# Two attentions of a three-block network: order of TensorE's steps, division on GpSimd, sink as a key column

## The chip, the cores and the metric

One Trainium2 chip, one of its cores. The metric is the device time of the one launch in microseconds; lower is better. The kernel is written in a low-level language: for each engine (TensorE, VectorE, ScalarE, GpSimd, SyncE) its own program, held together by counting semaphores.

## The reference, cut to what matters

Three blocks in a row. The first convolves, the second holds a windowed attention over 512 tokens and 256 context tokens, the third a sliding-window attention (6 heads), an attention over 256 memory tokens (4 heads) and a recurrent mixer; each is followed by a convolving feed-forward part. What the change touches, for one head of 64 (q, k, v), with a sink s:

```python
logits = q @ k.T * 64 ** -0.5              # + mask or bias, -inf outside the window
m = max(max(logits), s)
e = exp(logits - m)
p = e / (sum(e) + exp(s - m))              # the memory heads have no sink
out = p @ v
```

## The kernel before, in words

Weights stream in pieces from memory through SyncE's queue, are split into a high and a low part (ScalarE, GpSimd) and multiplied in three products each. Between these streams stand the two attentions: the first (ATT1) after the stream `qkv` and ahead of `wo`, the second (ATT2) after `w_in`, followed by the mixer's preparation (`rw_pre`).

An attention is a list of **units**: one block of 128 queries of one head. ATT1 has 64 units in 16 groups of 4 (`groups1`, L2250): for each of 4 key heads 4 blocks of queries, each with 4 query heads. A unit of the first and last block has 512 keys (256 of the window and 256 of the context), one of the middle blocks 640. So 512, 640, 640, 512 follow each other, four units each. ATT2 has 24 units in 4 groups of 6 (128 keys in the first group, then 256) and 16 units of the memory heads in 4 groups of 4, with 256 keys (`groups2`, L2670). The 128 columns more or less are those of the band.

What each engine does for a unit u:
- TensorE, `att_pe` (L1976): `scores` (L1979), in the fast 32-bit form, with the high and low part of the keys, the masks or the bias, into one of two pairs of PSUM banks. It waits until the exponential of u-2 is done (`att_p`). `turn` (L1987) transposes the probabilities in squares of 128 into one of three banks, a piece at a time. `values` (L2003) multiplies a whole group's transposed probabilities with the values, in full 32-bit form, with outputs of 64 rows in either half of the array; it is cut into four quarters, each in a step of its own.
- VectorE, `att_dve` (L2043): `negated` takes the maximum and multiplies it by -1/8 (in ATT1 with the sink as the other bound); `inverse` adds the sink's exponential in ATT1, takes the reciprocal and divides the row of probabilities; copies of transposed pieces marked "D"; `low`, the low part of a group's result.
- ScalarE, `att_act` (L2083): `exps`, in ATT1 the sink's exponential first, then that of the row, with its sum; copies of the pieces marked "A" (all in ATT1, every second unit in ATT2); `high_part` of a group's result.
- GpSimd has no part in it. Ahead of ATT2's stretch it has six operations of `rw_pre_pool` (L2940).

The order is written out by hand: each engine runs a loop over steps u, and the constants of L1943 say by how many steps a part lags behind the scores. TensorE's step u is: scores of u+2, `turn` of u-1, then a quarter of the values of a group whose last unit is u-2 to u-5. Each engine works through its queue in order.

ATT2's band units already carry the sink as two extra columns of the scores (`sk2`, L2562), of which one is used. In ATT1 the sink is a column of its own (`sinks`, `nsk`).

Of the kernel before, what the change touches and what calls it, by code (L numbers as in the profile page):

```python
# [6 lines left out]
P = 128  # L7
D = 1024
KD = D // P
SEQ = 512  # L10
# [5 lines left out]
HD = 64  # L16
TAPS = 31
# [77 lines left out]
def constants():  # L95
# [19 lines left out]

    sin = sin * np.repeat(np.array([-1, 1, 1, -1], np.float32), HD // 2)[:, None]
    q, k = np.arange(P)[:, None], np.arange(P)[None]
# [33 lines left out]
class Program:  # L151


    def __init__(self, nc, ctx, A):
# [42 lines left out]
        self.sm_max = at("sm_max", region(64), [4])  # L197
        self.sm_neg = at("sm_neg", region(64), [4])
        self.sm_sum = at("sm_sum", region(64), [4])
        self.sm_rd = at("sm_rd", region(64), [4])  # L200
        self.sm_e = at("sm_e", region(64), [4])
# [65 lines left out]
        self.nsk = nxt("nsk", [16])  # L267
# [5 lines left out]
        self.p1 = nxt("p1", [3, 648])  # L273
# [3 lines left out]
        self.p2 = nxt("p2", [3, 264])  # L277
# [100 lines left out]
def build_in(nc, ctx, A, out, stop):  # L378
# [77 lines left out]
    att_p = sem("att_p")  # L456
    att_n = sem("att_n")
# [1079 lines left out]
    zero_col = M.one[:, 2:3]  # L1537

# [386 lines left out]
    class Unit:  # L1925
# [5 lines left out]
        def __init__(self, scores, nk, parts, place, at=0, sink=None):  # L1931
            self.scores, self.nk, self.at, self.sink = scores, nk, at, sink
            self.parts, self.place = parts, place

# [6 lines left out]
    SCALE = HD ** -0.5  # L1941
    TURN_BANK, OUT_BANK = 4, 7
    TURN, VALUES, OUT_A, OUT_D, HIGH, LOW = 1, 2, 2, 3, 6, 7  # L1943

    class Attention:
# [26 lines left out]

        def turn_ps(self, j):
            return (TURN_BANK + j % 3) * 512

    def att_pe(pe, X, first=None):  # L1976
# [10 lines left out]
        def turn(u):  # L1987
            x = X.units[u]
            pe.wait_ge(att_n, done(X.u0 + u + 1))
            for m, (k0, nk, _) in enumerate(x.parts):  # L1990
# [7 lines left out]
                for k in range(0, nk, P):  # L1998
                    mm = pe.transpose(M.ps[:, X.turn_ps(j) + k:X.turn_ps(j) + k + P],
                                      X.p[:, u % 3, k0 + k:k0 + k + P], ident)  # L2000
                mm.then_inc(att_t, 1)

        def values(g, quarter):  # L2003
            grp, e = X.groups[g], X.last[g]
            if quarter == 0:
# [5 lines left out]
            for o, v, rhs, first, last in todo[quarter * len(todo) // 4:(quarter + 1) * len(todo) // 4]:  # L2011
                mm = pe.matmul(o, v, rhs, start=first, stop=last, skip_group_check=True)  # L2012
            if quarter == 3:
                mm.then_inc(att_o, 1)
# [1529 lines left out]
```

## Time and profile before

| what | value |
|---|---|
| median of three runs | 2412.74 us (2409.75 to 2416.72) |
| the profiled execution, its own time | 2414.43 us |
| its span | 2412.6 us |
| TensorE busy | 2258.1 us (94%) |
| VectorE, ScalarE, GpSimd busy | 1170.6, 994.5, 859.1 us |
| mean granted TensorE clock | 0.963 |

How to read it: busy times are of instructions, and TensorE's matmuls overlap, so its share is no measure of its speed. The loads of weights (PEld) give a better beat: one belongs to each matmul. A granted clock of 1.00 is 2.4 GHz, 0.50 is 1.2 GHz. `ps` is PSUM, `p` a row of probabilities, `pt` the transposed ones, `sm_...` the small columns of a row's maximum, sum and reciprocal.

### The profile page before, as it was taken

The numbers are of one execution on the slowest core, as the hardware profiler recorded it, in microseconds if no ns is written. First come the engines' busy times: TensorE is split into PE (matmuls) and PEld (weight loads), VectorE is DVE, ScalarE is ACT, GpSimd is POOL, SyncE is SP. The second block draws the span as 40 slices with busy tenths as digits, with TensorE's granted clock in tenths as the row PEclk, the third lists the DMA queues.
The fourth block names the chain that finished last, engine by engine and source line by source line (L and its number), as shares of the span: only waits on it lengthen the run. The fifth ranks groups of instructions, "written<-read, shape, count | busy, mean of one in ns | idle before, by whom it ended". The sixth has DMA issues, their size and how long they took to land.

```text
span 2412.6 us, 37223 instructions
## 1 busy us (share of the span) xinstructions
PE 2258.1 (94%) x14399; PEld 1868.9 (77%) x14399; DVE 1170.6 (49%) x2044; ACT 994.5 (41%) x1685; POOL 859.1 (36%) x449
## 2 busy tenths in 40 slices
PE   4999598999999998999989999989988889999998
PEld 3888487888888887877778888877746777878877
DVE  3699824332033325678433223458465436540541
ACT  5666544332133314588444324444353213441441
POOL 1699324223223324400244444433301113444443
PEclk8999898999999998999989999999888989999999
DMA  8778011222122221300123333332200002332332
GB/s 274 254 255 274 25 53 53 61 62 74 57 61 61 71 70 55 96 19 1 45 88 96 102 90 96 102 105 79 83 1 1 2 2 70 102 103 84 97 106 83
DMA packets 337730, 205.96 MB, mean 85 GB/s; under 512 B 5997, under 2 KB 335287, under 8 KB 337591
## 3 DMA queue, kind: packets, MB, share of 16 engines
q1 hardware_dynamic: 331915, 193.83, 26.9%
q10 hardware_dynamic: 5676, 10.24, 1.4%
q8 instruction: 93, 1.52, 0.3%
q14 instruction: 46, 0.38, 0.1%
HBM read 200.28 MB, written 2.19 MB: 84 GB/s over the span
## 4 chain that ended last, share of the span: by engine, by line
PE 72%; issue 11%; POOL 5%; DVE 5%; ACT 3%; DVEq 1%; SPq 1%; DMA 1%; ACTq 1%; POOLq 0%
PE ps L621 21%; PE ps L622 21%; PE ps L623 21%; POOL w_lo L548 2%; POOL pc L1608 2%; DVE ps L1576 1%; PE ps L894 1%; PE ps L1984 1%; PE ps L2012 1%; ACT w_hi L591 1%; DVE m L3214 1%; PE ps L3013 1%; DMA ada_x<-in_ada_w 1%; PE ps L1668 0%; SPq L772 0%
## 5 line engine op out<-in xcount | busy, mean ns | idle before, releaser
L548 POOL TENSOR_TENSOR w_lo<-raw,w_hi 128x1024 fp32r<-128x1024 f32 (+1 forms) x203 | 526.2, 2593 | 1073.4 <-ACT w_hi L591 1056.8
L621 PE MATMUL ps<-x_hi,w_hi 128*128 128x512 f32 (+1 forms) x1896 | 686.5, 362 | 35.1 <-DVE x_lo L1479 14.0
L622 PE MATMUL ps<-x_lo,w_hi 128*128 128x512 f32 (+1 forms) x1896 | 676.2, 357 | 0.0
L623 PE MATMUL ps<-x_hi,w_lo 128*128 128x512 f32 (+1 forms) x1896 | 674.9, 356 | 0.0
L591 ACT ACTIVATE w_hi<-raw 128x1024 fp32r<-128x1024 f32 (+1 forms) x251 | 280.6, 1118 | 615.8 <-PE ps L623 610.5
L621 PEld LDWEIGHTS ps<-x_hi,w_hi 128*128 128x128 f32 x1896 | 365.1, 193 | 100.0 <-issue 22.8
L622 PEld LDWEIGHTS ps<-x_lo,w_hi 128*128 128x128 f32 x1896 | 365.5, 193 | 50.0 <-issue 1.7
L623 PEld LDWEIGHTS ps<-x_hi,w_lo 128*128 128x128 f32 x1896 | 364.7, 192 | 50.5
L1858 DVE SCALAR_TENSOR_TENSOR f_a<-ps,prm,f_a 128x511 f32<-128x511 f32 (+2 forms) x176 | 116.2, 681 | 378.5 <-ACT f_b L1820 367.6
L621 PE MATMUL ps<-g_hi,w_hi 128*128 128x512 f32 (+1 forms) x704 | 256.8, 365 | 3.9 <-DVE g_lo L1867 1.7
L622 PE MATMUL ps<-g_lo,w_hi 128*128 128x512 f32 (+1 forms) x704 | 255.7, 363 | 0.0
L623 PE MATMUL ps<-g_hi,w_lo 128*128 128x512 f32 (+1 forms) x704 | 255.3, 363 | 0.0
L574 POOL TENSOR_TENSOR w_lo<-raw,w_hi 128x1024 fp32r<-128x1024 f32 x50 | 119.6, 2394 | 209.8 <-ACT w_hi L591 209.8
L1576 DVE SCALAR_TENSOR_TENSOR ps<-vp,prm,ps 128x512 f32<-128x512 f32 x320 | 169.4, 617 | 3.5 <-PE ps L956 3.5
L621 PEld LDWEIGHTS ps<-g_hi,w_hi 128*128 128x128 f32 x704 | 132.8, 189 | 26.7 <-DVE g_lo L1867 4.6
L623 PEld LDWEIGHTS ps<-g_hi,w_lo 128*128 128x128 f32 x704 | 132.7, 188 | 21.0
L622 PEld LDWEIGHTS ps<-g_lo,w_hi 128*128 128x128 f32 x704 | 132.8, 189 | 20.2
L1820 ACT ACTIVATE f_a<-ps,prm 128x512 f32<-128x512 f32 (+1 forms) x66 | 55.8, 845 | 211.0 <-PE ps L623 209.0
L621 PE MATMUL ps<-xg_hi,w_hi 128*128 128x512 f32 x352 | 137.7, 391 | 2.4 <-POOL w_lo L548 2.4
L1608 POOL TENSOR_TENSOR pc<-pc,pt 128x768 f32<-128x768 f32 x72 | 132.5, 1840 | 17.5 <-ACT pt L1597 10.6
L622 PE MATMUL ps<-xg_lo,w_hi 128*128 128x512 f32 x352 | 137.0, 389 | 0.0
L623 PE MATMUL ps<-xg_hi,w_lo 128*128 128x512 f32 x352 | 137.0, 389 | 0.0
(384 smaller groups left out, 2969.3 us busy)
## 6 DMA issues: line engine op xcount, KB each, us to landing
raw<-in_ffn_w_up SPq DMA_DIRECT2D x88, 512.0 KB, 3.8
ada_tail<-in_ada_w SPq DMA_DIRECT2D x22, 1024.0 KB, 7.4
raw<-in_ffn_w_down SPq DMA_DIRECT2D x32, 704.0 KB, 4.6
raw<-in_w_up SPq DMA_DIRECT2D x44, 512.0 KB, 3.8
ada_s<-in_ada_w SPq DMA_DIRECT2D x20, 1024.0 KB, 7.9
raw<-in_conv_w_pw SPq DMA_DIRECT2D x24, 512.0 KB, 6.3
raw<-in_w_down SPq DMA_DIRECT2D x16, 704.0 KB, 4.6
raw<-in_w_in SPq DMA_DIRECT2D x17, 512.0 KB, 3.9
```

The costliest lines, as they stand in the source:

```text
L548: pool.tensor_tensor(M.w_lo[:, slot, 0:K * P], M.raw[:, slot, 0:K * P], M.w_hi[:, slot, 0:K * P].bitcast(F32), ALU.subtract).then_inc(lo_r ...
L574: pool.tensor_tensor(M.w_lo[:, slot, 0:K * P], M.raw[:, slot, 0:K * P], M.w_hi[:, slot, 0:K * P].bitcast(F32), ALU.subtract).then_inc(lo_r ...
L591: act.activation(M.w_hi[:, slot, 0:K * P], M.raw[:, slot, 0:K * P], ACT.Copy).then_inc(hi_ready, 1)
L621: pe.matmul(o, wh, hi[:, k, t0:t0 + tn], start=first, stop=False)
L622: pe.matmul(o, wh, lo[:, k, t0:t0 + tn], start=False, stop=False)
L623: return pe.matmul(o, wl, hi[:, k, t0:t0 + tn], start=False, stop=last)
L894: mm = pe.matmul(M.ps[32 * q:32 * q + 32, at:at + P], M.sc32[:, k, :], weights[q // 2][:, k, q % 2 * P:(q % 2 + 1) * P], start=(k == 0), s ...
L1576: dve.scalar_tensor_tensor(out=o, in0=src, scalar=w, in1=o, op0=ALU.mult, op1=ALU.add)\
L1608: pool.tensor_tensor(acc, acc, M.pt[:, m % PT_RING, :], ALU.add).then_inc(pool_tap, 1)
L1820: ins = act.activation(dst[:, slot, 0:w], M.pair(pr, 0, w), ACT.Identity, scale=ffn_cols(b, zero_tap, t, hf, j), bias=ffn_cols(b, None, t, ...
L1858: ins = dve.scalar_tensor_tensor(out=dst[:, slot, o0:o1], in0=M.pair(pr, o0 + sh, o1 + sh), scalar=ffn_cols(b, tap, t, hf, j), in1=dst[:, ...
L1984: mm = pe.matmul(M.pair(u % 2, off, off + n), lhs, rhs, start=first, stop=True, skip_group_check=True)
```

## The change

- TensorE's step is now: a piece of values, `turn` of u-3, scores of u+2. The values of a group come in two pieces, in steps L+5 and L+6 for the group's last unit L.
- Lags: TURN 3 (1), OUT_A 3 (2), OUT_D 4 (3), VALUES 5 (2); HIGH 6 and LOW 7 stay. There are five rows of probabilities (3) and eight small columns (4).
- The factor 1/8 is put into the tables and scales of the queries, so that the exponential has a scale of 1 and the maximum is negated by the reduction itself.
- ATT1's sink becomes a column of the scores (one more matmul with two columns), as in ATT2; its exponential and the sum drop out.
- The reciprocals are taken for two units at once, every second step, and GpSimd divides (`att_pool`).
- In ATT1 the piece of the 256 context keys is copied by VectorE, that of the band by ScalarE.

```diff
-    TURN, VALUES, OUT_A, OUT_D, HIGH, LOW = 1, 2, 2, 3, 6, 7
+    TURN, OUT_A, OUT_D, VALUES, PIECES_V, HIGH, LOW = 3, 3, 4, 5, 2, 6, 7
...
-        for u in range(n_u + VALUES + 3):
+        for u in range(n_u + VALUES + PIECES_V):
+            for piece in range(PIECES_V):
+                for g in X.groups_at(u, VALUES + piece):
+                    values(g, piece)
+            if 0 <= u - TURN < n_u:
+                turn(u - TURN)
             if u + 2 < n_u:
                 scores(u + 2)
-            if 0 <= u - TURN < n_u:
-                turn(u - TURN)
-            for quarter in range(4):
-                for g in X.groups_at(u, VALUES + quarter):
-                    values(g, quarter)
...
         def negated(u):
-            x, b = X.units[u], u % 4
+            x, b = X.units[u], u % 8
             dve.wait_ge(att_s, done(X.u0 + u + 1))
-            dve.tensor_reduce(M.sm_max[:, b:b + 1], M.pair(u % 2, x.at, x.at + x.nk), AX.X, ALU.max)
-            dve.drain()
-            if x.sink:
-                dve.tensor_scalar(M.sm_neg[:, b:b + 1], M.sm_max[:, b:b + 1], -SCALE, x.sink[1], ALU.mult, ALU.min)\
-                    .then_inc(att_m, 1)
-            else:
-                dve.tensor_scalar(M.sm_neg[:, b:b + 1], M.sm_max[:, b:b + 1], -SCALE, None, ALU.mult).then_inc(att_m, 1)
+            dve.tensor_reduce(M.sm_neg[:, b:b + 1], M.pair(u % 2, x.at, x.at + x.nk), AX.X, ALU.max, negate=True)\
+                .then_inc(att_m, 1)
         def inverse(u):
-            x, b = X.units[u], u % 4
-            dve.wait_ge(att_p, done(X.u0 + u + 1))
-            if x.sink:
-                dve.tensor_tensor(M.sm_sum[:, b:b + 1], M.sm_sum[:, b:b + 1], M.sm_e[:, b:b + 1], ALU.add)
-                dve.drain()
-            dve.reciprocal(M.sm_rd[:, b:b + 1], M.sm_sum[:, b:b + 1])
-            dve.drain()
-            p = X.p[:, u % 3, 0:x.nk]
-            dve.tensor_scalar(p, p, M.sm_rd[:, b:b + 1], None, ALU.mult).then_inc(att_n, 1)
+            b = u % 8
+            dve.wait_ge(att_p, done(X.u0 + u + 2))
+            dve.reciprocal(M.sm_rd[:, b:b + 2], M.sm_sum[:, b:b + 2]).then_inc(att_r, 1)
...
             if u < n_u:
                 negated(u)
-            if 0 <= u - 1 < n_u:
-                inverse(u - 1)
             if 0 <= u - OUT_D < n_u:
                 bring_out(dve, dve.tensor_copy, X, u - OUT_D, "D", att_t, att_ed)
+            if u % 2 == 0 and 0 <= u - 2 < n_u:
+                inverse(u - 2)
...
-            if x.sink:
-                act.activation(M.sm_e[:, b:b + 1], M.sm_neg[:, b:b + 1], ACT.Exp, scale=1.0, bias=x.sink[0])
-            act.activation(X.p[:, u % 3, 0:x.nk], M.pair(u % 2, x.at, x.at + x.nk), ACT.Exp, scale=SCALE,
+            act.activation(X.slot(u)[:, 0:x.nk], M.pair(u % 2, x.at, x.at + x.nk), ACT.Exp, scale=1.0,
...
+    def att_pool(pool, X):
+        for u, x in enumerate(X.units):
+            pool.wait_ge(att_r, done((X.u0 + u) // 2 + 1))
+            p = X.slot(u)[:, 0:x.n_keys]
+            pool.tensor_scalar(p, p, M.sm_rd[:, u % 8:u % 8 + 1], zero_col, ALU.mult, ALU.add).then_inc(att_n, 1)
...
-                    scores += [(SEQ, CTX, q, M.k_hi[:, g, SEQ:TOK], True), (SEQ, CTX, q, M.k_lo[:, g, SEQ:TOK], False)]
+                    scores += [(SEQ, CTX, q, M.k_hi[:, g, SEQ:TOK], True), (SEQ, CTX, q, M.k_lo[:, g, SEQ:TOK], False),
+                               (TOK, 2, M.fr[:, P:2 * P], M.sk1[:, h, :], True)]
...
-                    heads.append(Unit(scores, nk, [(0, nb, "A"), (nb, CTX, "A")], place, at,
-                                      (M.sinks[:, h:h + 1], M.nsk[:, h:h + 1])))
+                    heads.append(Unit(scores, nk, [(0, nb, "A"), (nb, CTX, "D")], place, at))
...
             if name == "w_out":
                 low_stream(pool, name, 0, 2)
                 rw_pre_pool(pool)
+                att_pool(pool, ATT2)
...
+            if name == "wo":
+                low_stream(pool, name, 0, 2)
+                att_pool(pool, ATT1)
                 low_stream(pool, name, 2, 8)
```

Outside the attentions: the two last of the ten rotated tiles of `qkv` (the keys) take the factor back with scalar_tensor_tensor in place of tensor_tensor, the sinks of ATT1 are split once into a high and a low part (`sk1`, two small operations), the queries of ATT2 get their factor through the scale and bias of a square root, and the bias table is copied without a factor.

## Rows read from the trace of the kernel before

**Rows 1.** Busy time per engine and granted clock (PEclk) in four stretches.
```profile
1025.48:1169.22 143.74, 137.15 (x940) 99.42 (x940) 113.68 (x336) 116.79 (x339) 2.38 (x1) 0.98 0.03 9
1733.06:1797.16 64.10, 56.10 (x299) 36.74 (x300) 48.12 (x187) 32.39 (x108) 5.39 (x6) 0.88 0.03 9
1772.00:1775.00 3.00, 3.00 (x12) 1.34 (x12) 1.90 (x9) 1.32 (x5) 0.00 (x0) 0.52 0.02 5
1777.00:1788.00 11.00, 9.10 (x46) 4.79 (x45) 9.70 (x38) 6.72 (x22) 0.00 (x0) 1.00 0.00 1
```

**Rows 2.** Waits from 1040 to 1150: total, times, longest in us.
```profile
PEld ps L1984 <- issue: 16.5, 43, 0.4
```

**Rows 3.** TensorE's weight loads, first attention: start, us, count; scores L1984, transposes L1999, values L2012.
```profile
1041.68 0.19 PEld L1984 LDWEIGHTS ps<-k_hi,q 128*128 128x128 f32 x1 [0.62 <-ACTq L2095]
...
1042.50 0.57 PEld L1999 LDWEIGHTS ps<-kb,p 128*128 128x128 f32 x5
...
1093.48 0.20 PEld L2012 LDWEIGHTS ps<-pt,vt 128*64 128x64 f32 x4 [0.17 <-issue]
1094.06 0.19 PEld L1984 LDWEIGHTS ps<-k_hi,q 128*128 128x128 f32 x1 [0.39 <-ACTq L2095]
...
1095.29 0.62 PEld L2012 LDWEIGHTS ps<-pt,vt 128*64 128x64 f32 x6 [0.17 <-issue]
1096.29 0.19 PEld L1984 LDWEIGHTS ps<-k_hi,q 128*128 128x128 f32 x1 [0.38 <-issue]
...
1096.89 0.47 PEld L1999 LDWEIGHTS ps<-kb,p 128*128 128x128 f32 x4
```

**Rows 4.** The same: scores of unit 13, scores of unit 61, first product of wo.
```profile
1054.72 0.19 PEld L1984 LDWEIGHTS ps<-k_hi,q 128*128 128x128 f32 x1 [0.39 <-issue]
...
1154.58 0.19 PEld L1984 LDWEIGHTS ps<-k_hi,q 128*128 128x128 f32 x1 [0.39 <-issue]
...
1169.22 0.19 PEld L621 LDWEIGHTS ps<-x_hi,w_hi 128*128 128x128 f32 x1 [1.39 <-DVE x_lo L2071]
```

**Rows 5.** Second attention: a sink's matmul and what follows; units 16, 22, 39.
```profile
1750.92 0.19 PEld L1984 LDWEIGHTS ps<-sk,fr 128*128 128x128 f32 x1
1751.06 0.20 PEld L1999 LDWEIGHTS ps<-kb,p 128*128 128x128 f32 x2
...
1754.77 0.19 PEld L1984 LDWEIGHTS ps<-k_hi,pj_r 128*128 128x128 f32 x1 [0.35 <-issue]
...
1763.70 0.19 PEld L1984 LDWEIGHTS ps<-k_hi,pj_r 128*128 128x128 f32 x1 [0.35 <-issue]
...
1788.58 0.19 PEld L1984 LDWEIGHTS ps<-x_hi 128*128 128x128 f32 x1 [0.81 <-ACTq L2095]
```

**Rows 6.** Groups by form in both attentions: count | busy us, mean ns | idle before.
```profile
L2093 ACT ACTIVATE p<-ps,sm_neg 128x640 f32<-128x640 f32 x32 | 24.9, 779 | 0.0
L2049 DVE TENSOR_REDUCE sm_max<-ps 128x1 f32<-128x512 f32 x32 | 22.1, 689 | 12.7 <-PE ps L1984 12.4
L2093 ACT ACTIVATE p<-ps,sm_neg 128x512 f32<-128x512 f32 x32 | 21.7, 679 | 0.0
L2103 ACT ACTIVATE x_hi<-ps 128x256 fp32r<-128x256 f32 x16 | 6.2, 385 | 6.5 <-PE ps L2012 6.3
...
L2943 POOL TENSOR_SCALAR behind<-pj,prm,one 128x512 f32<-128x512 f32 x3 | 2.3, 766 | 0.4 <-DVE pj L2623 0.4
L2103 ACT ACTIVATE x_hi<-ps 128x384 fp32r<-128x384 f32 x4 | 2.0, 492 | 3.6 <-PE ps L2012 3.6
```

**Rows 7.** Timeline at the start of the second attention: rw_pre on GpSimd, a reduction.
```profile
1733.96 1.04 POOL L2945 TENSOR_TENSOR behind<-behind 128x512 f32<-128x512 f32 x1
...
1734.33 0.29 DVE L2049 TENSOR_REDUCE sm_max<-ps 128x1 f32<-128x129 f32 x1 [1.32 <-PE ps L1984]
...
1737.72 1.04 POOL L2945 TENSOR_TENSOR behind<-behind 128x512 f32<-128x512 f32 x1
```

**Rows 8.** Timeline: the copy behind the transposes of 1096.89.
```profile
1097.42 0.38 ACT L2098 ACTIVATE pt<-ps 128x256 f32<-128x256 f32 x1 [0.27 <-PE ps L1999]
```

More of the change, by code:

```diff
@@ L16 @@
 HD = 64
+SCALE = HD ** -0.5
 TAPS = 31
@@ L272, in __init__ @@
         o = self.mod_rows_at
-        self.p1 = nxt("p1", [3, 648])
+        p1 = nxt("p1", [3, 648])
+        self.p1 = [p1[:, i, :] for i in range(3)] + [t[:, :] for t in p1_more]
         self.pt1 = nxt("pt1", [2, 5 * 4 * P])
@@ L276, in __init__ @@
         o = r_s
-        self.p2 = nxt("p2", [3, 264])
+        p2 = nxt("p2", [3, 264])
+        self.p2 = [p2[:, i, :] for i in range(3)] + [at(f"p2_{3 + i}", r_raw + i * w + behind_8, [264])[:, :] for i in (0, 1)]
         self.pt2 = nxt("pt2", [2, 2 * 6 * P])
@@ L456, in build_in @@
     att_p = sem("att_p")
+    att_r = sem("att_r")
     att_n = sem("att_n")
@@ L1537, in build_in @@
     zero_col = M.one[:, 2:3]
+    eps_q_col = M.one[:, 4:5]
     VLAT, VCTX = PAD, SEQ + 3 * PAD
@@ L1925, in build_in, with __init__ @@
     class Unit:
-        def __init__(self, scores, nk, parts, place, at=0, sink=None):
-            self.scores, self.nk, self.at, self.sink = scores, nk, at, sink
+        def __init__(self, scores, nk, parts, place, at=0):
+            self.scores, self.nk, self.at = scores, nk, at
             self.parts, self.place = parts, place
+            self.n_keys = sum(n for _, n, _ in parts)
     class Group:
@@ L1971, in groups_at, with slot @@
             return [g for g, e in enumerate(self.last) if e + lag == u]
+        def slot(self, u):
+            return self.p[u % len(self.p)]
         def turn_ps(self, j):
@@ L1999, in turn, with values @@
                     mm = pe.transpose(M.ps[:, X.turn_ps(j) + k:X.turn_ps(j) + k + P],
-                                      X.p[:, u % 3, k0 + k:k0 + k + P], ident)
+                                      X.slot(u)[:, k0 + k:k0 + k + P], ident)
                 mm.then_inc(att_t, 1)
-        def values(g, quarter):
+        def values(g, piece):
             grp, e = X.groups[g], X.last[g]
-            if quarter == 0:
+            if piece == 0:
                 pe.wait_ge(att_ea, done(X.ea0 + X.brought_a[e]))
@@ L2010, in values @@
             todo = list(grp.products(X.pt[:, g % 2, :]))
-            for o, v, rhs, first, last in todo[quarter * len(todo) // 4:(quarter + 1) * len(todo) // 4]:
+            for o, v, rhs, first, last in todo[piece * len(todo) // PIECES_V:(piece + 1) * len(todo) // PIECES_V]:
                 mm = pe.matmul(o, v, rhs, start=first, stop=last, skip_group_check=True)
-            if quarter == 3:
+            if piece == PIECES_V - 1:
                 mm.then_inc(att_o, 1)
@@ L2214, in qkv_dve @@
             dve.wait_ge(rope_r, done(n + 1))
-            dve.tensor_tensor(M.gate[:, n % 2, 0:SEQ], ps, kf_cos, ALU.mult)
+            if n < 8:
+                dve.tensor_tensor(M.gate[:, n % 2, 0:SEQ], ps, kf_cos, ALU.mult)
+            else:
+                dve.scalar_tensor_tensor(out=M.gate[:, n % 2, 0:SEQ], in0=ps, scalar=1.0 / SCALE, in1=kf_cos,
+                                         op0=ALU.mult, op1=ALU.mult)
             dve.tensor_tensor(rope_ps(n)[a, :], ps[b, :], kf_sin[b, :], ALU.mult)
@@ L2222, in qkv_dve @@
             else:
-                dve.tensor_tensor(M.k_[:, n - 8, 0:SEQ], rope_ps(n), M.gate[:, n % 2, 0:SEQ], ALU.add).then_inc(rope_c, 1)
+                dve.scalar_tensor_tensor(out=M.k_[:, n - 8, 0:SEQ], in0=rope_ps(n), scalar=1.0 / SCALE,
+                                         in1=M.gate[:, n % 2, 0:SEQ], op0=ALU.mult, op1=ALU.add).then_inc(rope_c, 1)
             if n == 5:
-                dve.tensor_scalar(M.nsk[:, :], M.sinks[:, 0:16], -1.0, None, ALU.mult).then_inc(fr_ready, 1)
+                dve.wait_ge(fr_ready, done(1))
+                dve.scalar_tensor_tensor(out=M.sk1[HD:P, :, :], in0=M.sinks[HD:P, 0:16].unsqueeze(2)
+                                         .to_broadcast([HD, 16, 2]), scalar=1.0 / HD,
+                                         in1=M.sk1[HD:P, :, :].bitcast(F32), op0=ALU.mult, op1=ALU.subtract)\
+                    .then_inc(fr_ready, 1)
             if 1 <= n <= 8:
@@ L2663, in w_in_dve @@
                 for n in range(3):
-                    ins = dve.scalar_tensor_tensor(out=M.bias_lo[:, 2 * n:2 * n + 2, :], in0=halves(odd(BIAS_BANK[n])),
-                                                   scalar=1.0 / SCALE, in1=M.bias[:, 2 * n:2 * n + 2, :].bitcast(F32),
-                                                   op0=ALU.mult, op1=ALU.subtract)
+                    ins = dve.tensor_tensor(M.bias_lo[:, 2 * n:2 * n + 2, :], halves(odd(BIAS_BANK[n])),
+                                            M.bias[:, 2 * n:2 * n + 2, :].bitcast(F32), ALU.subtract)
                 V_S.mark(ins, "blo")
```

46 lines of the change are left out of this document (27 added, 19 removed).

## The prediction

> **What bounds the kernel now.** I read the stretches first, then the waits, the timeline of TensorE and the durations by form. The two attentions last 143.7 and 64.1 us of the span of 2412.6 [rows 1]. Outside them the change touches only a few small operations, so the answer lies in these 208 us. In the first one TensorE shows busy for 137 us, ScalarE for 117, VectorE for 114. In its middle 110 us TensorE's score loads pause for 16.5 us with nothing to wait for ("issue") [rows 2]: TensorE bounds it, with pauses of its own.
>
> The pauses have a pattern. A unit with 512 keys (A) takes 0.60 us of scores and 0.46 of transposes, then 0.17 of pause and a piece of value products; one with 640 (B) takes 0.82 and 0.57 [rows 3]. A piece of 4 instructions lasts 0.58 to the next load, one of 6 lasts 1.00: 0.42 per slot (the two column halves run beside each other) and 0.16 fixed. So a piece costs 0.33 us besides its products, where the tile shape goes to 128*64 and back. Sixteen units (8 A, 8 B, in 4 groups) come to 8 x 1.42 (scores) + 8 x 1.03 (transposes) + 16 x 0.33 + 20 slots x 0.42 = 33.3 us. Units 13 to 61 are three such periods: 99.86 us, 33.3 each [rows 4]. The sum holds.
>
> **The change on TensorE.** Two pieces per group in place of four save 8 x 0.33 = 2.6 us a period. The sink's column costs one more matmul per unit, 0.14 us from its load to the next in the second attention, which has it already [rows 5]: 2.2 us. A period is then 32.9: only 0.4 less.
>
> **The other engines.** VectorE loses the product with -1/8, the addition of the sink's exponential, half the reciprocals and the division; it gains the copy of the 256 context keys. ScalarE loses the sink's exponential and that copy. None of it is time where TensorE bounds. The division goes to GpSimd, idle here: 0.77 us for 512 elements in the same form [rows 6]. For 640 it is at least that and at most 0.96, in proportion. Against 1.8 us and more per unit it is covered and I take it at zero: the transposes wait two steps longer than before. Without cover it would show first in step L+8 (L the last unit of a group), where the pair's reciprocals stand some 1.5 us ahead of its first transposes; one division of 0.96 fits. VectorE is not slowed by it: its reduction of 129 elements at 1734.33 takes 0.29 while GpSimd works from 1733.96 on [rows 7].
>
> **The new wait.** With TURN and OUT_A at 3, ScalarE's step u is: exponential of u, copy of unit u-3. That copy needs the transposes which TensorE makes in its own step u, behind a value piece. The next exponential is queued behind the copy, and scores u+3 wait for that exponential. It decides in step L+6, where ScalarE also makes the high part. From the end of the transposes: 0.07 to the copy (transposes 1096.89 plus 0.46, copy 1097.42), copy 0.33 (0.43 for 384), high part 0.39, exponential with its accumulator 0.77 or 0.87, and 0.08 to TensorE [rows 6, 8]: 1.64 (A) or 1.84 (B). TensorE meanwhile has one unit's scores and transposes, 0.74 + 0.46 = 1.20 or 0.96 + 0.57 = 1.53. It stalls for 0.44 or 0.31 us, 0.38 a group, 1.5 a period. Bounds: zero, if ScalarE turns out to have more room; 0.9 a group, if each of the five links comes 0.1 later. In steps without values the loop of scores, reduction (0.69) and exponential needs 1.25 us a unit (A), which TensorE needs too: no more stall.
>
> **First attention.** Per period -0.4 + 1.5 = +1.1, three times: +3.3. Start: values begin in step 8, not 5, and the chain to the exponential lacks two small instructions; followed with these durations, unit 13 comes 2.4 us earlier. End: what was put off has to be done. Unit 61 to the first product of wo lasts 14.6 us before [rows 4]. After, three units' scores, five units' transposes, the last pieces of groups 13, 14 and 15, one stall, and the last high and low part make 16: +1.4. Sum +2.3.
>
> **Second attention.** Six operations of rw_pre stand on GpSimd ahead of the first division and end at 1738.76 [rows 7]: unit 6 comes 0.5 us later; then the later start of the values gives back, and unit 16 comes 1.8 us earlier in all. Six band units take 8.93 us (units 16 to 22) [rows 5]. After: on TensorE 6 x 0.79 + 2 x 1.17 = 7.1; the wait above costs 1.0 (one unit is only 0.79 of work, against 0.07 + 0.33 + 0.49 for the high part of 384 [rows 6] + 0.64 + 0.25 until the other engines are in step); smaller waits for copies and reductions 0.6: 8.7, so -0.2. The four units of a memory head are only 4.2 us of TensorE, but ScalarE's chain of copy, high part, exponential, copy, exponential makes 6.3. Units 22 to 39 come to 25.1 us against 24.9 [rows 5], which hold a stretch at half clock (0.52) [rows 1] that I take as gone. Sum -1.8 - 0.2 + 0.2 and an unchanged end, rounded: -1.6, as followed.
>
> The scales folded into tables, the keys' sums as scalar_tensor_tensor and the copy of the sinks lie beside the weight products of qkv and w_in: zero, at most 0.5 us without that cover.
>
> **Sum.** 2.3 - 1.6 = +0.7 us. The profiled execution took 2414.4 us (span 2412.6 and 1.8 around it), 1.7 above the median of three runs, 2412.74. From the median: **2413.4 us**. A measurement can tell about 0.3%, 7.2 us, from no change, so this is no change. Its own range is 2407 to 2420: with the bounds of the stalls, 14 groups x -0.38 or +0.5.
>
> **Rivals.** *TensorE alone* (faster): ScalarE is never late. Then the stalls go: 14 x 0.38 = 5.3 in the first attention, 3 x 1.6 and 3 x 2.1 in the second, 16.4 in all: 2397. For it: ScalarE has 27 us free in the first [rows 1]. Against: its order, not its load, holds it. It decides once half of this is won, below 2405. Chance 0.26.
>
> *Half clock in the memory groups* (slower): TensorE there would pause for 2 us in 6.3. The trace shows that it comes in this very place: from 1772 to 1775 the grant is 0.52, the lower of the two levels [rows 1]. At it two pieces of 1.17 last 2.0 and the other 1.8 us up to twice as long: +3.5 a group, 2424 with three groups. It decides from two groups on. Against: from 1777 to 1788 memory groups ran at the full clock, with weight loads busy for only 4.8 of 11 us [rows 1]. Chance 0.16. The Trainium skill (TensorE: Matmul & The Clock Gate, A second HAM failure mode: psum-queue depth-cycling) says that TensorE, when it pauses shortly and often between groups of matmuls, swings between its two clocks; by that rule this would be the likelier rival.
>
> **Numbers.** Forecast 0.58, rivals 0.26 and 0.16. Of the forecast little passes 0.3% on either side. Faster 0.27, same 0.56, slower 0.17. The range of 2402 to 2422 leaves out the farther half of both rivals.
>
> **What would show it.** Right: a period of 16 units near 34.4 us; pieces of 1.00 and 1.43 with the same pauses; once a group, in step L+6, scores that wait 0.3 to 0.5 us for ScalarE; GpSimd at some 0.8 us a unit with nobody waiting for it; unit 13 two us earlier, wo two us later; a memory group of 6.3 us. Wrong: a period below 33, transposes that wait for GpSimd, or a longer stretch at half clock in the second attention than before.

## The result and the profile after

The changed kernel took 2418.01 us (median of 20 runs, 2408.91 to 2420.88), the kernel before beside it 2411.57. The ratio is 1.0017 with a 95% interval of 1.0009 to 1.0025, or about +4 us (the two medians alone lie 6.4 us apart, because the changed kernel's times fall into two clusters, 5 below 2412 and 15 above 2416): within the 0.3% that the prediction calls no change, and inside its range of 2402 to 2422. The profiled execution took 2419.05 us (span 2417.2).

So the number was right. The parts were not: the first attention became shorter, not longer, and what the change lost it lost where the prediction had put nothing. From the first instruction of each stage on TensorE to the next, in the profiled executions:

| stage | before | after | forecast | found |
|---|---|---|---|---|
| up to the first attention | 1025.48 | 1026.94 | 0 | +1.5 |
| first attention | 143.74 | 141.62 | +2.3 | -2.1 |
| wo and feed-forward to w_in | 430.64 | 431.37 | 0 | +0.7 |
| w_in | 133.20 | 136.51 | 0 | +3.3 |
| second attention | 63.99 | 64.69 | -1.6 | +0.7 |
| the rest | 615.55 | 616.07 | 0 | +0.5 |
| span | 2412.6 | 2417.2 | +0.7 | +4.6 |

The two attentions of the changed kernel, stretches as in [rows 1] (us, then busy time of PE, PEld, DVE, ACT, POOL, the granted clock, the DMA's share and GB/s):

```profile
1026.94:1168.56 141.62, 134.71 (x1004) 108.82 (x1004) 80.53 (x176) 83.08 (x211) 54.17 (x65) 0.96 0.03 8
1736.44:1801.13 64.69, 54.88 (x298) 38.05 (x298) 28.14 (x87) 30.64 (x107) 26.69 (x46) 0.85 0.03 9
```

VectorE and ScalarE lost 33 and 34 us in the first one, and the attention became 2 shorter: neither bounded it by its load. Its waits from 1040 to 1150, as [rows 2] (waiter, releaser, total, times, longest):

```profile
PEld ps L2008 <- issue: 6.9, 18, 0.4
PEld ps L1993 <- ACTq L2092: 5.2, 19, 0.4
PEld ps L2008 <- POOL p L2114: 3.1, 8, 0.4
```

Before, the pauses had no releaser, 16.5 us of them ahead of the scores alone; in the same stretch 10.0 are left (first and third row), and the scores (L1993) wait for ScalarE's exponential (L2092) instead. The wait on GpSimd (L2114) is in the place of the pause behind a value piece and of its length, so it costs nothing.

Weight loads of the changed kernel, as [rows 3] and [rows 4]: the second step with values (piece, transposes, scores), the two steps behind it, then scores of units 13 and 61 and the first product of wo.

```profile
1054.84 0.19 PEld L1993 LDWEIGHTS ps<-k_hi,q 128*128 128x128 f32 x1 [0.43 <-ACTq L2092]
...
1090.80 1.05 PEld L2021 LDWEIGHTS ps<-pt,vt 128*64 128x64 f32 x10
1092.24 0.53 PEld L2008 LDWEIGHTS ps<-kb,p 128*128 128x128 f32 x5 [0.38 <-issue]
1092.74 0.19 PEld L1993 LDWEIGHTS ps<-k_hi,q 128*128 128x128 f32 x1
...
1093.45 0.53 PEld L2008 LDWEIGHTS ps<-kb,p 128*128 128x128 f32 x5
1094.34 0.19 PEld L1993 LDWEIGHTS ps<-k_hi,q 128*128 128x128 f32 x1 [0.35 <-ACTq L2092]
...
1095.65 0.19 PEld L1993 LDWEIGHTS ps<-k_hi,q 128*128 128x128 f32 x1 [0.19 <-ACTq L2092]
...
1152.15 0.19 PEld L1993 LDWEIGHTS ps<-k_hi,q 128*128 128x128 f32 x1 [0.19 <-ACTq L2092]
...
1168.56 0.19 PEld L626 LDWEIGHTS ps<-x_hi,w_hi 128*128 128x128 f32 x1 [1.39 <-DVE x_lo L2070]
```

Units 13 to 61 take 97.31 us, 32.4 a period (forecast 34.4; before 33.3). Read the distances. A piece of ten loads to the transposes takes 1.44 (forecast 1.43). Five transposes to the next scores take 0.50 at 1092.24, but 0.89 at 1093.45: a stall of 0.39, where the forecast had 0.44 in this very place, the step behind ScalarE's step L+6. Over a period this first stall is 0.39 twice, where the scores are those of 512 keys, and 0.27 twice, where they are those of 640. What holds it is ScalarE's queue:

```profile
1092.83 0.49 ACT L2095 ACTIVATE pt<-ps 128x384 f32<-128x384 f32 x1 [1.57 <-PE ps L2008]
1093.22 0.38 ACT L2100 ACTIVATE x_hi<-ps 128x256 fp32r<-128x256 f32 x1
1093.48 0.70 ACT L2090 ACTIVATE p<-ps,sm_neg 128x513 f32<-128x513 f32 x1
1094.05 0.21 ACT L2090 ACTIVATION_READ_ACCUMULATOR p<-ps,sm_neg 128x1 f32 x1
```

ScalarE waits 1.57 us for the transposes, then copies, makes the high part, and only then comes the exponential that the scores of 1094.34 need: the five links of the prediction. The next step adds 0.22 that it did not have (0.61 for 0.39), in two of a period's four groups; in the other two it adds nothing.

GpSimd by forms in the first attention, for the forecast of 0.77 and at most 0.96:

```profile
L2114 POOL TENSOR_SCALAR p<-p,sm_rd,one 128x640 f32<-128x640 f32 x32 | 27.8, 880 | 35.0 <-DVE sm_rd L2065 35.0
L2114 POOL TENSOR_SCALAR p<-p,sm_rd,one 128x512 f32<-128x512 f32 x32 | 24.4, 773 | 46.4 <-DVE sm_rd L2065 46.4
```

### The profile page after: what moved, and what is told of

Its sections match the earlier page's. It is cut to its first block, busy times and chain, and to the rows that moved or that the text cites. A ratio compares the mean times of both kernels' runs of the same rounds, so it can differ in the third digit from the quotient of the medians.

```text
span 2417.2 us, 36779 instructions
## 1 busy us (share of the span) xinstructions
PE 2260.5 (94%) x14463; PEld 1884.5 (78%) x14463; DVE 1117.2 (46%) x1784; ACT 960.1 (40%) x1558; POOL 933.6 (39%) x554
## 4 chain that ended last, share of the span: by engine, by line
PE 79%; POOL 5%; DVE 5%; issue 4%; ACT 3%; ACTq 1%; DVEq 1%; DMA 1%; SPq 1%; POOLq 0%
PE ps L626 22%; PE ps L627 21%; PE ps L628 21%; PE ps L1993 3%; PE ps L2021 2%; POOL pc L1614 2%; PE ps L2008 2%; POOL w_lo L553 2%; DVE ps L1582 1%; PE ps L899 1%; ACTq L2092 1%; ACT w_hi L596 1%; DVE m L3230 1%; PE ps L3029 1%; DMA ada_x<-in_ada_w 1%
## 5 line engine op out<-in xcount | busy, mean ns | idle before, releaser
L1614 POOL TENSOR_TENSOR pc<-pc,pt 128x768 f32<-128x768 f32 x72 | 132.7, 1844 | 17.4 <-ACT pt L1603 10.5
```

The source lines that it names most:

```text
L1614: pool.tensor_tensor(acc, acc, M.pt[:, m % PT_RING, :], ALU.add).then_inc(pool_tap, 1)
```

## The experiments

My theory after the profile, before the runs: TensorE's own beat of a period is 30.6 us, and 1.8 of stalls stand on it, by ScalarE's order; outside the attentions nothing changed but the stretches at half clock. (The trace's record of the clock gives their lengths; a window's PEclk shows them as a share.) The rivals: the stalls come from the shortness of the steps without values; and the edits outside the attentions cost the missing time. All kernels were timed in five rounds beside the kernel before, 5 to 12 runs each: e1 to e4, e5 to e8 and e9 to e12 beside 34, 23 and 28 runs of it, with medians of 2411.76, 2412.74 and 2411.27, so medians of different groups compare by their ratios. "Period" is a third of the time from unit 13 to unit 61 in the kernel's own profile; the attentions run from first to first instruction as above.

| kernel | median us | ratio to before, 95% interval | period | first | second |
|---|---|---|---|---|---|
| changed, again (e3) | 2418.58 | 1.0022 (1.0013 to 1.0031) | 32.4 | 141.56 | 62.89 |
| before, again (e12) | 2411.69 | 1.0001 (0.9990 to 1.0011) | 33.3 | 143.78 | 63.46 |
| e1 high part first | 2406.82 | 0.9973 (0.9962 to 0.9983) | 31.7 | 138.65 | 57.31 |
| e4 VectorE divides | 2422.78 | 1.0038 (1.0027 to 1.0050) | 35.6 | 153.10 | 64.83 |
| e5 no sink in the first | 2412.06 | 0.9989 (0.9979 to 1.0000) | 32.2 | 139.54 | 63.16 |
| e6 transposes, values | 2411.67 | 0.9986 (0.9975 to 0.9996) | 32.5 | 142.06 | 59.21 |
| e7 four pieces | 2434.22 | 1.0081 (1.0065 to 1.0097) | 36.3 | 155.30 | 70.76 |
| e8 high first, one piece | 2397.95 | 0.9929 (0.9914 to 0.9945) | 30.3 | 133.43 | 56.12 |
| e9 high first, pair cut | 2403.25 | 0.9961 (0.9948 to 0.9974) | 30.9 | 135.48 | 57.64 |
| e2 outside edits alone | 2415.47 | 1.0011 (1.0000 to 1.0023) | 33.3 | 143.82 | 64.52 |
| e10 the first's share | 2415.61 | 1.0018 (1.0009 to 1.0028) | | 143.78 | 64.08 |
| e11 the second's share | 2412.43 | 1.0004 (0.9994 to 1.0014) | | 143.30 | 62.55 |

### e1: is it the order in ScalarE's queue?

```diff
+            for g in X.groups_at(u, HIGH):
+                high_part(g)
             if 0 <= u - OUT_A < n_u:
                 bring_out(act, copy, X, u - OUT_A, "A", att_t, att_ea)
-            for g in X.groups_at(u, HIGH):
-                high_part(g)
```

> The changed kernel with one edit: in ScalarE's step the high part of a group stands ahead of the copy, not behind it. In the changed kernel's profile ScalarE is late for the scores by 0.2 to 0.4 us in the two steps behind a group's pieces, 1.8 us in a period of 16 units (32.4 us). Theory A (the late exponential is the copy plus the high part queued ahead of it, as the prediction had it): the high part then runs while TensorE still transposes, the chain is shorter by 0.39, the stall of step L+6 goes and that of L+7 shrinks, a period takes 30.9 to 31.3 us and the first attention is 4 to 6 us shorter; with the clock's stretches as they are, median near 2413. Rival B (the stall is the short work of the two steps without values, whatever ScalarE's order): the period stays at 32.2 to 32.5 and the median at 2418.

The same step in its timeline of ScalarE:

```profile
1087.80 0.38 ACT L2100 ACTIVATE x_hi<-ps 128x256 fp32r<-128x256 f32 x1 [1.09 <-PE ps L2021]
1088.27 0.49 ACT L2095 ACTIVATE pt<-ps 128x384 f32<-128x384 f32 x1
1088.66 0.68 ACT L2090 ACTIVATE p<-ps,sm_neg 128x513 f32<-128x513 f32 x1
```

The high part now runs beside the transposes. The transposes that took 0.89 to the next scores take 0.61, and the period falls by 0.74 to 31.7: less than the 1.1 to 1.5 expected, since 0.1 to 0.3 of stall stays in six of the eight steps without values, 1.0 in all. The first attention becomes 3.0 us shorter, the second 5.6 to 7.4 (two profiles of the changed kernel, with one and two stretches at half clock there that e1's lacks, some 1.5 us each). Theory A holds, with a smaller size in the first attention; the second, where the chain is long against TensorE's work, gains most even without these stretches. That gain the expectation had not counted: its median was 2413, measured 2406.82. Against the kernel before, this order is 0.27% faster.

### e4: was GpSimd's division worth anything?

```diff
-            dve.reciprocal(M.sm_rd[:, b:b + 2], M.sm_sum[:, b:b + 2]).then_inc(att_r, 1)
+            dve.reciprocal(M.sm_rd[:, b:b + 2], M.sm_sum[:, b:b + 2])
+            dve.drain()
+            for v in (u, u + 1):
+                p = X.slot(v)[:, 0:X.units[v].n_keys]
+                dve.tensor_scalar(p, p, M.sm_rd[:, v % 8:v % 8 + 1], None, ALU.mult).then_inc(att_n, 1)
```

> The changed kernel with the division back on VectorE: behind the two reciprocals, every second step, it divides both rows itself (0.49 and 0.55 us each in the kernel before); GpSimd has no part in the attentions. VectorE's work a unit rises from about 1.3 to 1.8 us against 2.0 us of the beat. Theory A (GpSimd's part is needed, since the next reduction is queued behind two divisions and the scores' exponential behind it): the period in the first attention rises from 32.4 to 33.5 to 36 us, the median by 4 to 14 us. Rival B (VectorE has room enough, the division's place doesn't matter): the period stays within 0.3 us of 32.4 and the median at 2418.

VectorE in one group:

```profile
1092.54 0.15 DVE L2065 RECIPROCAL sm_rd<-sm_sum 128x2 f32<-128x2 f32 x1
1092.77 1.02 DVE L2069 TENSOR_SCALAR p<-p,sm_rd 128x640 f32<-128x640 f32 x2
1093.69 0.69 DVE L2058 TENSOR_REDUCE sm_neg<-ps 128x1 f32<-128x513 f32 x1
```

The reduction stands behind two divisions of 1.02 us, the exponential behind the reduction, and scores wait up to 1.0 us once a group. The period rises by 3.2 us to 35.6, the first attention by 11.5. The median rises by only 4.2 over e3, since these runs were granted more clock (0.960 to 0.967, e3's 0.958 to 0.961); how far that moves a time is measured under e12, and at equal clock the rise is about 11. So the cover that the prediction counted at zero is not free by itself: with these lags the division is free on GpSimd only.

### e5: what does the sink's column cost?

```diff
-                nk = CTX + nb + 1
+                nk = CTX + nb
...
-                scores += [..., (SEQ, CTX, q, M.k_lo[:, g, SEQ:TOK], False),
-                               (TOK, 2, M.fr[:, P:2 * P], M.sk1[:, h, :], True)]
+                scores += [..., (SEQ, CTX, q, M.k_lo[:, g, SEQ:TOK], False)]
```

> The changed kernel without the sink of the first attention: its column of the scores (one matmul of two columns a unit) and the 513th or 641st key are left out, so the outputs lack the sink there. From the changed kernel's profile a unit's scores take 0.71 (A) and 0.94 us (B) to the next load against 0.59 and 0.82 before: 0.12 a unit. Theory A (TensorE's beat counts in the eight steps with values, ScalarE's chain in the others): 8 x 0.12 = 1.0 us comes off the 32.4 of a period, the other eight give nearly nothing since the stall grows by what the scores lose; 31.3 to 31.6 a period, the first attention 3.5 to 5 us shorter. Rival B (TensorE's beat counts everywhere): 1.9 us off the period, 30.5, and 8 us off the attention.

e5 computes another result: its outputs lack the sink. Both theories miss: the period falls by only 0.2 us. Another 1.4 us come at the start, but there its profile has 6.8 us at half clock and both of the changed kernel have 10.2, so they are not the sink's alone. Its weight loads, a step without values and one with them:

```profile
1091.87 0.19 PEld L1993 LDWEIGHTS ps<-k_hi,q 128*128 128x128 f32 x1 [0.42 <-ACTq L2092]
...
1092.46 0.47 PEld L2008 LDWEIGHTS ps<-kb,p 128*128 128x128 f32 x4
1093.19 0.19 PEld L1993 LDWEIGHTS ps<-k_hi,q 128*128 128x128 f32 x1 [0.26 <-ACTq L2092]
...
1093.97 1.05 PEld L2021 LDWEIGHTS ps<-pt,vt 128*64 128x64 f32 x10
```

Scores take 0.78 to a value piece, with the sink 0.79: the same. To transposes they take 0.59 without and 0.71 with it. So in the steps with values the small matmul fits into a pause that is there without it (0.19), and in the others its 0.12 is taken back by the wait for ScalarE. The 2.2 us that the prediction charged a period are 1.0 on TensorE without its waits and 0.2 in the balance. The rows also price a piece behind scores where no sink fills the pause: 0.19 ahead of it (0.78 for 0.59) and 0.16 inside, 0.35.

### e6: what does the place of the piece cost?

```diff
+            if 0 <= u - TURN < n_u:
+                turn(u - TURN)
             for piece in range(PIECES_V):
                 for g in X.groups_at(u, VALUES + piece):
                     values(g, piece)
-            if 0 <= u - TURN < n_u:
-                turn(u - TURN)
```

> The changed kernel with the transposes of u-3 ahead of the piece of values, not behind it. In the kernel before transposes followed by a piece took 0.63 and 0.74 us, in the changed kernel transposes followed by scores 0.38 and 0.50, and scores followed by a piece 0.08 more than scores followed by transposes: so a piece behind transposes costs 0.17 more than one behind scores. Theory A: on TensorE a period gains 8 x 0.17 = 1.3 us; but ScalarE copies while the piece runs, so that the stall of step L+6 shrinks from 0.3 to at most 0.1 and that behind it too: 1.2 us less. The period stays at 32.0 to 32.8. Rival B (the place of the piece is free, only the number of pieces counts): TensorE gains nothing, the stall goes all the same, 30.9 to 31.3.

```profile
1091.34 0.53 PEld L2008 LDWEIGHTS ps<-kb,p 128*128 128x128 f32 x5
1092.03 1.05 PEld L2021 LDWEIGHTS ps<-pt,vt 128*64 128x64 f32 x10 [0.17 <-issue]
1093.47 0.19 PEld L1993 LDWEIGHTS ps<-k_hi,q 128*128 128x128 f32 x1 [0.38 <-issue]
```

Five transposes to a piece take 0.69, against 0.50 to scores, and the piece the same 1.44. Scores lose the 0.08 that they took longer ahead of a piece, so this place costs 0.11 to 0.12 a piece, not the 0.17 expected: 1.0 us a period, and the stalls fall from 1.8 to 0.9. The period stays (32.5), as theory A had it: what the place costs, the shorter stall gives back. The second attention is 3.7 to 5.5 us shorter; one or two stretches at half clock that this profile lacks are 1.5 to 3 of that.

### e7: two pieces or four?

```diff
-    TURN, OUT_A, OUT_D, VALUES, PIECES_V, HIGH, LOW = 3, 3, 4, 5, 2, 6, 7
+    TURN, OUT_A, OUT_D, VALUES, PIECES_V, HIGH, LOW = 3, 3, 4, 5, 4, 8, 8
```

> The changed kernel with a group's values in four pieces, in steps L+5 to L+8, and the high and low part in step L+8. Theory A (a piece costs 0.16 inside and 0.08 ahead of it, beside its products; the steps without values are where ScalarE is late): TensorE's beat rises from 30.6 to 30.6 + 8 x 0.24 = 32.5 us a period; the stalls of the short steps (1.8) go, but a new one comes in step L+9, where the values wait for the low part behind a copy and the high part: 0 to 0.6 a group. Period 32.5 to 34.9. Rival B (a piece costs 0.41 wherever it stands, as the kernel before has it): 30.6 + 3.3 = 33.9 without a stall, and up to 36.3 with it.

```profile
1097.03 0.20 PEld L2021 LDWEIGHTS ps<-pt,vt 128*64 128x64 f32 x4
1097.61 0.53 PEld L2008 LDWEIGHTS ps<-kb,p 128*128 128x128 f32 x5 [0.39 <-issue]
...
1101.62 0.23 PEld L2021 LDWEIGHTS ps<-pt,vt 128*64 128x64 f32 x4 [0.55 <-issue]
...
1102.99 0.19 PEld L1993 LDWEIGHTS ps<-k_hi,q 128*128 128x128 f32 x1 [0.34 <-ACTq L2092]
```

The sum of its rows without waits is 32.5 a period, as theory A has it, and a piece is 0.24 dearer than its products. The stall was underestimated: 0.95 a group instead of at most 0.6. The first piece of the next group waits 0.3 to 0.6 for the low part, and the scores behind it 0.3 to 0.6 more for ScalarE, which puts the period outside theory A's range. The total, 36.3, is also what rival B allowed at most, so it is the rows that tell them apart, not the total.

### e8 and e9: versions that beat both, and why a cut matters

e8 is e1 with one piece a group (VALUES, PIECES_V, HIGH, LOW = 5, 1, 5, 6). e9 is e1 with this:

```diff
-            for o, v, rhs, first, last in todo[piece * len(todo) // PIECES_V:(piece + 1) * len(todo) // PIECES_V]:
+            at = [i * (len(todo) // 2) // PIECES_V * 2 for i in range(PIECES_V + 1)]
+            for o, v, rhs, first, last in todo[at[piece]:at[piece + 1]]:
```

> The version with the high part ahead of the copy (31.7 us a period, median 2406.8), and in it the values of a group in one piece, in step L+5, with the high part in L+5 and the low part in L+6. Theory A (a piece costs 0.24 beside its products): TensorE's beat falls by 4 x 0.24 = 1.0 us to 29.6; but three steps of four are now short ones, 1.1 us (A) and 1.3 (B) of TensorE against a chain of ScalarE (exponential, copy, 1.05 to 1.3 us), so that 0.1 to 0.3 of a stall comes in each of them: period 31.0 to 32.3, the median 2404 to 2409. Rival B (stalls as in the version it builds on, 1.1 a period): 30.7, median 2402 to 2404.

> The version with the high part ahead of the copy (two pieces, 31.7 us a period, first attention 138.65 us), with each group's products cut only between pairs: ten products as 4 and 6 in place of 5 and 5; in the second attention the two products of a memory group come together, in step L+6. The rows so far: a piece of 8 loads (4 products) 1.01 us, of 10 loads (5) 1.44, of 16 (8) 1.87, of 20 (10) 2.31. Theory A (the products of the two column halves run beside each other in pairs, so that an odd cut leaves two halves alone): pieces of 1.01 and 1.44, so 0.42 less in each of the 8 groups with ten products, 0.84 a period, of which a stall of ScalarE may take back up to half: period 30.9 to 31.3, first attention 1.7 to 3.4 us shorter. Rival B (a piece costs a fixed pause and each load the same): nothing changes, 31.6 to 31.8.

The piece of a whole group in e8, then a piece of four products in e9:

```profile
1084.94 1.93 PEld L2021 LDWEIGHTS ps<-pt,vt 128*64 128x64 f32 x20
1087.25 0.53 PEld L2008 LDWEIGHTS ps<-kb,p 128*128 128x128 f32 x5 [0.38 <-issue]
```

```profile
1084.78 0.63 PEld L2022 LDWEIGHTS ps<-pt,vt 128*64 128x64 f32 x8
1085.79 0.53 PEld L2008 LDWEIGHTS ps<-kb,p 128*128 128x128 f32 x5 [0.38 <-POOL p L2115]
```

e9 does what was computed: its pieces take 1.01 and 1.45 us where e1 has 1.44 twice, and the period falls by 0.84 to 30.86, the whole of 2 x 0.42: nothing went to a stall. Every piece is 0.16 us and 0.42 a pair of products, within 0.05: 0.58, 1.01, 1.44 (five products, three pairs), 1.87, 2.31. The Trainium skill (TensorEngine Tiling (Array Packing), Key Properties) says that different tiles can load and multiply in parallel; by that rule an odd product in a piece leaves one column half idle, and the traces agree with 0.42 us.

e8 has no odd cut and half the pieces: the sum without waits is 29.0 (8 x 0.71 + 8 x 0.94 + 4 x 0.08 for scores, 8 x 0.39 + 8 x 0.495 for transposes, 2 x 2.31 + 2 x 1.88 for pieces), the period 30.3, so 1.3 of stalls stay, where theory A had 1.4 to 2.7 on a beat of 29.6. The median of 2397.95 is 0.71% below the kernel before and the best version here. It was below what both theories gave, since neither had counted the pairs.

### e2, e10, e11: the edits outside the attentions

e2 is the kernel before with all edits outside the attentions and none inside; e10 has the rotated tables, the keys scaled back and sk1 (the first attention's), e11 the square roots' scales, the bias table and the sinks of the second. The core of e10:

```diff
+    cos, sin = cos * np.float32(SCALE), sin * np.float32(SCALE)
...
-                dve.tensor_tensor(M.k_[:, n - 8, 0:SEQ], rope_ps(n), M.gate[:, n % 2, 0:SEQ], ALU.add).then_inc(rope_c, 1)
+                dve.scalar_tensor_tensor(out=M.k_[:, n - 8, 0:SEQ], in0=rope_ps(n), scalar=1.0 / SCALE,
+                                         in1=M.gate[:, n % 2, 0:SEQ], op0=ALU.mult, op1=ALU.add).then_inc(rope_c, 1)
```

> The kernel before with the edits outside the attentions alone: tables scaled by 1/8, keys scaled back by scalar_tensor_tensor, sk1 made but not used, square root and bias with their new scales; the attentions keep their order, lags, division and sink. Theory A (these edits lie beside the weight products and cost nothing; the changed kernel's extra microseconds outside the attentions are stretches at half clock): same as before within 0.5 us, and the time from the first stage to the first attention as before. Rival B (they cost the 1.5 us that the first attention starts later, and more in w_in): 2 to 5 us slower than before.

> The kernel before with the first attention's share of the edits outside the attentions: scaled tables, keys scaled back, sk1 made but not used; the second attention and w_in are as before. The kernel with all of these edits had a median of 2415.5 us against 2411.8. Theory A (the edits cost TensorE nothing; stretches at half clock fall otherwise): stages outside half-clock stretches keep their lengths within 0.3 us, and any difference of the medians is the stretch in w_in at 1630 being there more often (w_in 104.2 us with 6.8 us of it, 101.4 without). Rival B (the two longer operations on the keys and the two small ones delay the first attention): the first attention starts 0.5 to 1.5 us later in every profile and the median is 2413 or more.

> The kernel before with the second attention's share of those edits: scales and biases of the square roots, the bias table and the sinks without factor. No instruction is added. Theory A (nothing but the chance of a stretch at half clock in w_in): median 2411 to 2413. Rival B (the share of the 3.7 us lies here): 2414 to 2416, and it shows between the start of w_in and the second attention.

From the last pause ahead of qkv (the four loads that follow a wait of 1.8 us for n_t) to the first attention the kernel before takes 92.63 and 92.59 us in its two profiles and e11 92.55. With the first attention's edits it is 92.76 to 93.07 in eight profiles, and 93.29 to 93.51 in three: 0.1 to 0.9, mostly 0.3, where the prediction had "at most 0.5". But e10's median is 4.3 us above that of before, while e11's interval holds 1. Neither expectation explains this: rival B is right on the medians of e2 and e10, but its mechanism accounts for 0.9 us in e10's profile and 0.4 in e2's, of 4, and in e10's profile the part of w_in behind its first 32 us takes 101.4, as in the kernel before, without a stretch at half clock.

### e3, e12: the same kernels again

> The changed kernel, unchanged, for a second profile and more times. In 20 runs it took either 2409 to 2411.5 us (5 times) or 2416.6 to 2421 (15 times). Theory A (the two values are stretches of TensorE at half clock outside the attentions; the first profile, 2417.2 us, has one of 6.8 us in w_in that the kernel before lacks): a profile of the lower value lacks that stretch, both have a period of 32.4 us in the first attention, and stage lengths differ only where the granted clock differs. Rival B (the attentions themselves run in two ways, with more or fewer waits): the period differs between profiles by over 0.5 us.

> The kernel before, unchanged, against itself, for a second profile and for what this comparison gives when nothing differs. Theory A (the time varies by stretches of TensorE at half clock, about one run in five lies at 2416 or more): ratio within 0.999 and 1.001, period 33.3 us, and where the profile is above 2416 it has the stretch of 6.8 us in w_in that the changed kernel's has. Rival B (the edits outside the attentions cost 3 us or more by themselves): this profile never has that stretch.

Nine microseconds of w_in, from 32 us after its start on, of three executions: the kernel before in its first profile, the changed kernel, the kernel before again.

```profile
1631.86:1640.86 9.00, 7.98 (x35) 6.29 (x35) 7.47 (x8) 3.01 (x6) 4.33 (x3) 1.00 0.43 117
```

```profile
1631.93:1640.93 9.00, 7.74 (x20) 5.85 (x21) 7.00 (x6) 1.79 (x4) 4.23 (x2) 0.62 0.42 117
```

```profile
1632.26:1641.26 9.00, 7.71 (x27) 6.00 (x28) 7.02 (x6) 1.84 (x4) 4.26 (x2) 0.81 0.40 117
```

The work is the same, the clock is 1.00, 0.62 and 0.81, and w_in takes 133.20, 136.51 and 135.03 us. So the 3.3 us of the first table are not a cost of any instruction: the kernel before has a stretch in the same place in e12, half as long (3.4 us, where the expectation had 6.8), and e11, which adds no instruction to it, has the whole 6.8. The period does not move (32.4 in both profiles of the changed kernel, 33.3 in both of before), so rival B of e3 falls; its profile, 2414.52, has a stretch of 3.4 us in this place, where theory A had none.

What moves is the granted clock of a whole execution, and that can be counted. Each timed run lists its mean clock; those of the changed kernel (31) and those of the kernel before that ran beside e1 to e12 (85):

| mean clock | before: runs, mean us | changed: runs, mean us |
|---|---|---|
| 0.957, 0.958 | 0 | 6, 2419.1 |
| 0.959 | 3, 2419.8 | 13, 2418.8 |
| 0.960 | 8, 2418.3 | 5, 2417.7 |
| 0.961 | 10, 2417.1 | 2, 2415.6 |
| 0.962 | 7, 2414.8 | 0 |
| 0.963 | 20, 2412.1 | 2, 2411.2 |
| 0.964 | 11, 2411.3 | 3, 2410.5 |
| 0.965, 0.966 | 26, 2410.6 | 0 |

At an equal clock the changed kernel is 0.6 to 1.5 us faster. The same comparison gives, on average over the runs, +0.3 for e12 (nothing differs; +0.8 against its own rounds alone, so a value is good to about 1 us), +1.9 for e10, +2.0 for e2, +1.1 for e11, +10.5 for e4 and -8.4 for e1. By that the edits outside cost up to 2 us, of which a stage shows only those in qkv, and the attentions would win 2 to 3, a difference that no run isolates. And 26 of the changed kernel's 31 runs lie at 0.961 or below, of the kernel before 21 of 85. So the 6.4 us between the medians go with less granted clock. Part of it is in the attentions and is its own: 10 us at half clock in the first 28 us of the first attention (twice the missing share, 2 x 0.18 x 27.9), where before has 7 (2 x 0.12 x 29.2). That stretch is 10.2 us in eight of the nine profiles with the new order (6.8 in e5), and 6.8 in four of the five with the old one (3.4 in e11):

```profile
1025.48:1054.72 29.24, 24.63 (x158) 20.08 (x158) 20.94 (x62) 23.39 (x62) 2.38 (x1) 0.88 0.13 37
```

```profile
1026.94:1054.84 27.90, 23.66 (x155) 21.55 (x155) 13.79 (x28) 16.35 (x36) 10.18 (x11) 0.82 0.13 37
```

The other part of its own is a stretch at the end of the second, below. Why the stretches outside the attentions come more often is open. e10, which has only the edits of qkv, has no run above 0.964 either, though e2, which has them too, has three; a shift alone, without the edits, was not tried.

## Why the prediction was right, and where it was not

**TensorE's beat: wrong, by 2.2 us a period.** Step: the sum with 8 x 1.03 for transposes, 0.33 a piece and 0.14 a sink's matmul, all read in the old order and applied to the new one. Transposes were entered with the duration of their loads, 0.46 and 0.57; followed by scores they take 0.38 and 0.50 to the next load, where followed by a piece they took 0.63 and 0.74 [rows 3]. That is 1.2 us less than the sum had. The sink's matmul takes 0.12 in the eight steps without values and nothing in the others: 1.0 for 2.2, another 1.3 less. A piece by itself was priced about right (0.35 in e5 for 0.33), 0.3 more over the eight. The rows without waits sum to 8 x 0.71 + 8 x 0.94 + 8 x 0.08 (scores) + 8 x 0.385 + 8 x 0.495 (transposes) + 4 x 1.01 + 4 x 1.44 (pieces) = 30.7, against 32.9 in the prediction. The prices were measured in the old order and carried into one where the neighbour is another.

**The new wait: right.** Place, cause and size: 0.39 measured against 0.44 (units of 512 keys), 0.27 against 0.31 (640), 1.3 a period against 1.5, and e1, which undoes only the queueing, gains in both attentions. The 0.22 in the step behind it, in two groups of four, was missing: 1.8 a period instead of 1.5.

**First attention.** Steady part -2.55 for +3.3: all of it the beat. Start -1.3 for -2.4: it has 3 us more at half clock, worth 1.5 at most (an estimate, if TensorE bounds throughout; no run isolates it). End +1.8 for +1.4. Sum -2.1 for +2.3.

**GpSimd: right.** 773 and 880 ns, and nobody waits for it beyond a pause that is there anyway. e4 shows what its cover is worth: 11.5 us.

**Second attention.** Units 0 to 16: -1.8, as forecast (21.71 to 19.91; in e12 and e3 21.25 to 19.50). Band units: 8.3, forecast 8.7. Units 22 to 39: 25.36, forecast 25.1 without a stretch at half clock. That they meet is luck: e3, which has none there, takes 23.95, a memory group is 5.3 to 6.0 us for the forecast 6.3, and the kernel before's order without a stretch takes 23.4 to 23.6 (e2, e10, e11), so like for like this part costs 0.4 to 0.6. (The prediction's terms here sum to -1.8; it carried -1.6.) "An unchanged end" failed, by 2.6 us. The end before, after, and in e5 (same order in this attention):

```profile
1788.58:1797.05 8.47, 5.78 (x19) 1.95 (x19) 4.57 (x14) 3.08 (x8) 0.00 (x0) 1.00 0.00 0
```

```profile
1790.02:1801.13 11.11, 7.31 (x22) 2.50 (x21) 3.06 (x7) 3.35 (x9) 1.82 (x4) 0.85 0.00 0
```

```profile
1783.64:1793.22 9.58, 5.78 (x22) 2.17 (x21) 3.06 (x7) 3.35 (x9) 1.35 (x3) 1.00 0.00 0
```

1.1 us are the longer tail of lags, which the prediction had counted for the first attention and forgot for the second; 1.5 are a stretch at half clock.

**The rivals.** *TensorE alone* had the forecast's beat of 32.9, as wrong as there, and no stalls, where 1.8 a period were measured; e1, e8 and e9 take part of them away by another order, and e8's 2398 is near its 2397 by a beat and a cut that it did not have. *Half clock in the memory groups* came, in small: the two profiles of the changed kernel have two and one such stretches among the memory groups and their end, the two of the kernel before one each; e1, e6, e8 and e9, whose pauses there are shorter, have none, and e7 with the longest has three. But e2, e10 and e11, with the kernel before's order and pauses, have none either, and e4 and e5, with the changed kernel's order, two and one: the order does not settle it alone. A stretch cost some 1.5 us (25.36 - 23.95, 11.11 - 9.58), not 3.5, and did not decide. The rule of the Trainium skill that the prediction cites (TensorE: Matmul & The Clock Gate, A second HAM failure mode: psum-queue depth-cycling) agrees with the new orders' count and not with the old order's, one and none with the same pauses; no run here isolates it.

**The total** was thus right by luck, with errors that cancel: -4.4 in the first attention, +2.3 in the second, and about +6 outside, where the prediction allowed 0.5. Of these six, 0.7 stand in qkv (93.29 for 92.63) and 3.3 are the stretch in w_in, which another execution of the same kernel (e3) has half as long; the other 2 are spread and not settled.

## What to carry to other kernels

Price a pause by the pair of neighbours that makes it, not by the instruction it stands beside, and count products in the units that really run together: moving values ahead of transposes saved 0.12 us a piece (e6), an odd cut cost 0.42. When an engine is late in one step of a cycle, look at its own queue first: putting the high part ahead of a copy, which waits anyway, was worth more (11.8 us of median against e3) than the whole rewrite. And before 3 us are explained, run the same kernel again and compare at equal granted clock.

## What was not expected of the hardware

- A two-column matmul between scores and a value piece costs nothing (0.79 us with it, 0.78 without), and 0.12 between scores and transposes (0.71, 0.59).
- Identical work takes 101.4, 102.8 or 104.2 us (the part of w_in behind its first 32 us), by a stretch at half clock of 0, 3.4 or 6.8 us behind the same pause of TensorE. In all fourteen profiles that stretch is missing where the one at the start of w_in (near 1595) lasted 6.8 us, and there where that lasted 10.2. Where it is missing, the earlier one began 33.5 to 33.6 us ahead of the first load behind that pause, and 36.4 to 36.8 where it is there.
- Edits that lengthen qkv by 0.3 to 0.9 us (e10) go with 4.3 us of median, 1.9 at equal clock, good to about 1. The cause stays open.
